# Ten token copies moved from ScalarE to GpSimd behind a semaphore of their own

## The reference, cut to what matters

```
h = _rms(x, e_norm)
proj = h @ e_w_in
u, z_s5, q, k, v, z_da = split(proj)
uf = u.reshape(bsz, seq, 64, 16)
xr = einsum('blgh,gph->blgp', uf, bbr)      # and xi with bbi
hr, hi = associative_scan(...)               # h_t = a * h_(t-1) + x_t
y  = einsum('blgp,ghp->blgh', hr, c_re) - einsum(..., hi, c_im)
y  = gelu(y + d * u); y = y * sigmoid(y @ w_glu + b_glu)
```

## Time and profile before

| what | value |
|---|---|
| median of 3 runs | 940.35 us (939.56 to 941.47) |
| the profiled execution's own time | 940.36 us |
| its span, first to last instruction | 938.6 us |
| PE busy | 928.1 us (99%) |
| DVE, ACT busy | 590.9 us (63%), 586.3 us (62%) |
| POOL busy | 114.0 us (12%) |
| granted TensorE clock | 1.00 |

### The profile page before, as it was taken

How to read it: one execution, slowest core, us unless ns; L and a number is a source line. 1 busy time by engine, 2 the same in 40 slices (tenths; PEclk the granted TensorE clock), 3 DMA queues, 4 the chain that set the end, 5 groups by cost and what they waited for, 6 DMA issues and landing times.

```text
span 938.6 us, 15807 instructions
## 1 busy us (share of the span) xinstructions
PE 928.1 (99%) x5885; PEld 789.9 (84%) x5885; DVE 590.9 (63%) x937; ACT 586.3 (62%) x979; POOL 114.0 (12%) x141
## 2 busy tenths in 40 slices
PE   7999999999999999999999999999999999999998
PEld 7998788888889999888888888888888888888886
DVE  5687889798896756755545555654555555555553
ACT  4689989889898546554454655466456645555332
POOL 2100002030020100000022430310022002200000
PEclk9999999999999999999999999999999999999999
DMA  8787654746455565656999985769999766654662
GB/s 292 197 184 226 209 170 155 197 130 186 144 158 158 152 237 188 210 179 181 167 177 191 196 234 156 201 163 169 171 158 174 197 171 182 176 162 157 222 213 80
DMA packets 125512, 170.67 MB, mean 182 GB/s; under 512 B 20358, under 2 KB 65675, under 8 KB 125195
## 3 DMA queue, kind: packets, MB, share of 16 engines
q1 hardware_dynamic: 109008, 164.52, 67.0%
q10 hardware_dynamic: 16442, 5.33, 2.3%
HBM read 167.05 MB, written 2.77 MB: 181 GB/s over the span
## 4 chain that ended last, share of the span: by engine, by line
PE 91%; ACT 5%; issue 1%; DVE 1%; DMA 1%; SPq 0%; ACTq 0%
PE bank L524 23%; PE bank L526 23%; PE bank L525 23%; PE bank L551 4%; PE bank L553 4%; PE bank L552 4%; ACT wh L1034 2%; ACT early L1101 2%; PE bank L669 1%; PE bank L769 1%; PE bank L795 1%; PE bank L752 1%; PE bank L661 1%; PE bank L594 1%; DMA res<-in_x 1%
## 5 line engine op out<-in xcount | busy, mean ns | idle before, releaser
L1042 DVE TENSOR_TENSOR wl<-raw,wh 128x1024 fp32r<-128x1024 f32 x295 | 361.9, 1231 | 261.7 <-ACT wh L1034 260.7
L1034 ACT ACTIVATE wh<-raw 128x1024 fp32r<-128x1024 f32 x295 | 311.4, 1058 | 183.7 <-PE bank L526 119.3
L524 PE MATMUL bank<-wh,xh 128*128 128x512 f32 x768 | 307.2, 400 | 0.0
L526 PE MATMUL bank<-wh,xl 128*128 128x512 f32 x768 | 300.1, 391 | 0.0
L525 PE MATMUL bank<-wl,xh 128*128 128x512 f32 x768 | 299.4, 390 | 0.0
L526 PEld LDWEIGHTS bank<-wh,xl 128*128 128x128 f32 x768 | 144.1, 188 | 31.1
L524 PEld LDWEIGHTS bank<-wh,xh 128*128 128x128 f32 x768 | 144.4, 188 | 28.8 <-issue 0.2
L525 PEld LDWEIGHTS bank<-wl,xh 128*128 128x128 f32 x768 | 144.5, 188 | 27.7
L524 PE MATMUL bank<-wh,yh 128*128 128x512 f32 x256 | 100.5, 393 | 0.0
L526 PE MATMUL bank<-wh,yl 128*128 128x512 f32 x256 | 99.8, 390 | 0.0
L525 PE MATMUL bank<-wl,yh 128*128 128x512 f32 x256 | 99.7, 389 | 0.0
(11 more groups left out here) (321 smaller groups left out, 1006.3 us busy)
## 6 DMA issues: line engine op xcount, KB each, us to landing
raw<-in_o_w_in SPq DMA_DIRECT2D x128, 512.0 KB
raw<-in_e_w_in SPq DMA_DIRECT2D x130, 256.0 KB, 3.8
raw<-in_e_w_out SPq DMA_DIRECT2D x32, 512.0 KB
raw<-in_o_w_out SPq DMA_DIRECT2D x32, 512.0 KB
raw<-in_e_w_in SPq DMA_DIRECT2D x31, 512.0 KB
raw<-in_s_w_glu SPq DMA_DIRECT2D x8, 512.0 KB
res<-in_x SPq DMA_DIRECT2D x8, 256.0 KB, 6.5
scr<-p_rows SPq DMA_DIRECT2D x32, 64.0 KB, 3.2
```

Of the source, the lines that this page charges most:

```text
L524: nc.tensor.matmul(o, l_hi, w_hi, start=first, stop=False)
L526: mm = nc.tensor.matmul(o, l_lo, w_hi, start=False, stop=last)
L1034: nc.scalar.activation(wh[:, j % RING, :], raw[:, j % RING, :], ACT.Copy).then_inc(hi_done, 1)
L1042: nc.vector.tensor_tensor(wl[:, j % RING, :], raw[:, j % RING, :], wh[:, j % RING, :].bitcast(F32), ALU.subtract).then_inc(lo_done, 1)
```

## The change

The ten last copies (half 1, k = 6 to 15) leave ScalarE's list: `setup` issues none from slot 6 on. They enter GpSimd's list as `tensor_copy` behind the `c_n` copies and ahead of `step(0)`, each waiting for the one before. GpSimd waits for `c_twice` and for the second count of `acc_free[1]` first. The last one raises the new semaphore `u4_late`, and GpSimd itself waits for it. ScalarE's half 1 now gives its count of `u4_done` at k = 5. TensorE waits for `u4_late` as well for S5 blocks 2 and 3, the third and fourth pair.

```diff
@@ s5_in_x on TensorE
                     pe.wait_ge(u4_done, i // 2 + 1)
+                    if i >= DA_PAIRS // 2:
+                        pe.wait_ge(u4_late, 1)
@@ chunk_tokens on ScalarE
-                if k == 15:
+                if k == (15, 5)[half]:
                     ins.then_inc(u4_done, 1)
@@ setup on ScalarE
-                for k in (10 + 2 * s, 11 + 2 * s) if s < 6 else (16 + s,):
+                for k in (10 + 2 * s, 11 + 2 * s) if s < 6 else ():
                     chunk_tokens(k // 16, k % 16)
@@ GpSimd's list
             ins.then_inc(c_twice, 1)
+            pool.wait_ge(c_twice, 1)
+            pool.wait_ge(acc_free[1], 2)
+            for k in range(6, 16):
+                s, q = k // 4, k % 4
+                src = uz[32 * q:32 * q + 32, 4:8, :].rearrange("p k (c s) -> p k c s", s=HOP)[:, :, :, HOP - 1 - s]
+                dst = u4[32 * s:32 * s + 32, 16:32, :].rearrange("p (k q) c -> p k q c", q=4)[:, :, q, :]
+                ins = g.tensor_copy(dst, src)
+                if k == 15:
+                    ins.then_inc(u4_late, 1)
+                    pool.wait_ge(u4_late, 1)
+                else:
+                    link(ins)
             for i in range(DA_PAIRS + 1):
                 step(i)
```

More of the change, by code:

```diff
@@ L322, in build @@
         tab_ang, tab_abs, tab_done = (sem(n) for n in ("tab_ang", "tab_abs", "tab_done"))
-        u4_done, slopes = sem("u4_done"), sem("slopes")
+        u4_done, u4_late, slopes = sem("u4_done"), sem("u4_late"), sem("slopes")
         cc_done, ca_done, dd_done, steps_done, group_done = (sem(n) for n in
```

## The result

| | before | changed |
|---|---|---|
| median of 16 runs | 940.79 us (939.56 to 941.70) | 942.24 us (940.35 to 944.36) |
| profiled execution, its span | 940.36, 938.6 us | 942.78, 941.1 us |
| POOL, ACT busy | 114.0, 586.3 us | 127.6, 579.8 us |

The ratio is 1.0015, 95% interval [1.0008, 1.0022]: slower by 0.75 to 2.1 us, the median by 1.45. The forecast was +1.8.

The account below looks back on a forecast made before the run. TensorE was taken to bound the kernel. Eight holds of VectorE (3.84 us) less 0.50 hidden and 0.13 cover make TensorE 3.2 us late; less the 1.41 gain, 940.36 + 1.8 = 942.2 us, 8-in-10 range 938.9 to 944.2.

Parts of the forecast that it names:

- What bounds the kernel: TensorE, busy 928.1 of 938.6 us: only what starts it earlier or later counts; one wait of size, 1.4 us at s5_in_x.
- What is taken from ScalarE: Ten copies of 0.666 us off ScalarE's list; s5_near starts at 110.0 instead of 111.91 us, TensorE's whole wait goes, gain 1.41.
- the second spread: On ScalarE, slot 14's spread, at 106.41 us before, can start once VectorE's input is ready, taken as staying at 105.85.
- What one copy costs: On GpSimd, 0.61 us per strided copy: 0.36 for 256 elements plus 0.25 for the 16-byte step; limits 0.36 and 0.84.
- third rival: No change: the step costs half as much again, 0.49 us a copy, hold 0.36, 941.2 us; chance 0.12.
- What the copies cost VectorE: GpSimd copies and two-input VectorE operations alternate, whoever comes second waiting; each copy holds VectorE for 0.48 us.
- The hold: Time each GpSimd copy keeps VectorE's next operation waiting: 0.61 - 0.13 = 0.48 us, eight times 3.84, 0.5 of it hidden.
- the cover: VectorE's unit parts end 0.13 and 0.14 us before TensorE starts their units; 0.13 us was taken off the cost.
- The sum: Cost 3.84 - 0.50 - 0.13 = 3.2 us on TensorE, gain 1.41 beside it: net +1.8, 942.2 us; chance 0.50.
- The signs: Copies between 67.4 and about 81 us, 128x512 operations over 1.1 us, two TensorE idle pieces of about 1.6, no wait at L769.
- The first (no hold): Rival: copies don't hold VectorE where it matters, or the held time is hidden; 938.95 us, 0.15% faster; chance 0.18.
- The second (0.84 us a copy): Rival: copies cost per element what the two-input form costs, 0.84 us and more, eight times on VectorE; 944.0 us; chance 0.20.

Follow-up runs that it names:

- c2_cost: Kernel before, ScalarE keeping all 32 copies, with GpSimd also making the ten into spare columns at the changed kernel's place: 943.90 us against 940.53, ratio 1.0035.
- c1_gain: Changed kernel with the ten GpSimd copies left out, zeros written long before in their part of u4: 939.43 us against 940.53, ratio 0.9990.
- c6_memset: Changed kernel with the ten GpSimd copies replaced at their place by ten memsets that only write: 939.54 us against 941.11, ratio 0.9982.
- c9_four: Changed kernel with only the copies of slots 8, 9, 14 and 15 on GpSimd, behind lo_done 24: 939.71 us against 941.11, ratio 0.9982.

## Why the prediction was right

**What bounds the kernel.** This was right. TensorE's start times carry all: 2.99 us lost and 1.58 won give 1.41, and the median moved by 1.45.

**What is taken from ScalarE.** The wait goes whole, as forecast, and the size was a little small: 1.41 us forecast, 1.58 found. 1.48 of it lies at the wait itself (from unit 0 to unit 1 of step 1: 5.50 us before, 110.20 to 115.70; 4.02 after, 114.10 to 118.12), and about 0.1 ahead of L580, which the forecast left out. One premise failed without harm. The forecast let the second spread start 0.56 us earlier, since its input from VectorE was to stay at 105.85 us. TensorE is 4.00 us later in the changed kernel, and counted back by that, this input was there at 104.97 (the second L1805 starts at 108.28 and takes 0.69), and the spread started 1.40 us earlier, at 109.01 - 4.00 = 105.01. So the room left over at the end was larger, too: `s5_near` waits 0.39 us for TensorE and still ends at 116.03, 1.0 us ahead of L771 at 117.04, where 0.5 was forecast. Why the input came earlier was not studied.

**What one copy costs.** This was right: 0.61 us forecast from a contiguous copy and ScalarE's price for the step, 0.642 recorded; without the step 0.36 forecast, 0.399 recorded. The third rival's half more on the streaming part (0.49 us in all) falls short of the 0.642: by the difference of the two, the step adds 0.24 to the 0.30 us of streaming (0.399 less the 0.10 of the one-column memset), four fifths.

**What the copies cost VectorE.** The mechanism was right: one copy between any two operations, eight of them ahead of the second unit part. The hold was put at 0.48 us and measured at 0.44 (1.13 - 0.69) where VectorE's operation doesn't depend on the one before. Two errors met in it: the copy was taken 0.03 us too short, and what goes off its duration is 0.20 us, not 0.13. Behind an operation whose result is waited for, 0.32 and 0.34 us are left of the hold (1.01 - 0.69 and 1.56 - 1.22), so 0.12 and 0.10 are hidden, near the 0.12 forecast. From the end of the first unit part to that of the third VectorE took 9.46 us (69.55 to 79.01) instead of 6.37 (68.55 to 74.92), 3.09 more; the sum had 3.84 - 0.50 = 3.34. Of the cover, 0.09 us was used up and not 0.13: TensorE starts unit 5 0.14 us behind the end of VectorE's part before and 0.05 behind it after. Together TensorE lost 2.99 us, against 3.21 forecast.

**The sum.** It said +1.8 and the traces say +1.4, since both terms were off by 0.2 us in the same direction, the cost too high and the gain too low. "The last two copies come where ScalarE, not VectorE, sets the pace" was right: TensorE's offset to before stays 4.00 us from unit 5 to unit 12. The signs came as listed, but for the size of two: the two pieces of idle time are 1.23 and 1.26 us instead of 1.6, though the two units come 1.47 and another 1.52 us later, because the transposes ahead of a unit, which before ran on into its first matmul (74.70 + 0.60 against 75.06), now end ahead of it. And the third operation of 128x512 took 1.01 us, not over 1.1.

**The rivals.** The first (no hold) falls by c2_cost; that its time, 938.95, was about reachable is shown by c1_gain, c6_memset and c9_four, where nothing held VectorE ahead of unit 5. The second (0.84 us a copy) falls by the 0.642, and the third by the same and by the 2.99 us lost; by time alone its 941.2 is not excluded.

## What to carry to other kernels

An idle GpSimd is not free room: here each of its plain copies of 0.64 us held the next VectorE operation with two inputs in SBUF for 0.44 us. So look for the stretch in which VectorE has gaps, and move no more copies than the gaps hold. And before work is moved off an engine, find the last wait of that engine ahead of the late result: here two copies behind it gave 1.48 us, while eight, of which only one stood behind it, gave 0.70.

## What had not been expected of the hardware

Ten GpSimd memsets of 0.52 us beside two-input VectorE operations cost these nothing (0.68 to 0.69 us), while copies of 0.64 us cost 0.44 each. A GpSimd copy of 32x256 elements takes 0.40 us from neighbouring elements and 0.64 from every fourth one (16 bytes).
